# Step order in a two-block transformer kernel: one VectorE step per expert, gathered results in a split pair, ln2's norm ahead of the overflow branch

## What is computed

```python
for i in range(DEPTH):                      # first layers
    mix = token_mixers(x, ...)              # diff attention + dsa attention
    x = layer_norm(ALPHA * x + mix, ln1)
    ffn = hierarchical_moe(x, ...)          # 4 groups x 8 experts, 2 of one group per token
    ple = sigmoid(x @ w_ple_gate[i]) * (p[i] @ w_ple[i])
    x = layer_norm(ALPHA * x + ffn + ple, ln2)
for l in range(DEPTH):                      # second layers
    x = x + hybrid_mixer(rms_norm(x), ...)  # mla + moba + retention branches, gated
    x = x + squared_relu_mlp(rms_norm(x), w_up, w_down)
return rms_norm(x)
```

## Time and profile before

| | us |
|---|---|
| median of 3 runs (2105.99 to 2107.63) | 2106.68 |
| the profiled execution | 2105.99 |
| its span in the trace | 2104.2 |
| TensorE busy | 1964.6 |
| VectorE busy | 1410.0 |
| ScalarE busy | 1073.0 |
| GpSimd busy | 94.5 |

### The profile page before, as it was taken

The page is one execution under the profiler, slowest core; times in us unless marked ns, Lnnn a source line. Parts: engine busy times, 40 slices in busy tenths (PEclk is TensorE's granted clock), DMA queues, the critical chain, the costliest instruction groups (busy, mean ns, idle before and its releaser), DMA issues.

```text
span 2104.2 us, 31210 instructions
## 1 busy us (share of the span) xinstructions
PE 1964.6 (93%) x12616; PEld 1779.6 (85%) x12616; DVE 1410.0 (67%) x2278; ACT 1073.0 (51%) x1662; POOL 94.5 (4%) x88
## 2 busy tenths in 40 slices
PE   7889989999989799989999799999999899999998
PEld 6779878998877798779988689998999789998997
DVE  5765768888756766688887556667444666675444
ACT  4444446776634344467776254444444455444443
POOL 1000010000010000100000000000100000001001
PEclk9989899999989899899999799999999999999999
DMA  7425239999724243199998153344555443344552
GB/s 256 140 81 216 93 122 406 405 413 375 285 79 142 100 176 133 55 411 399 415 382 332 39 190 121 121 160 147 194 180 193 145 161 139 107 179 158 190 191 81
DMA packets 60152, 426.65 MB, mean 203 GB/s; under 512 B 6849, under 2 KB 7233, under 8 KB 9440
## 3 DMA queue, kind: packets, MB, share of 16 engines
q1 hardware_dynamic: 59040, 421.65, 53.2%
q0 software_dynamic: 384, 1.72, 0.3%
q10 hardware_dynamic: 576, 1.19, 0.2%
HBM read 423.49 MB, written 1.05 MB: 202 GB/s over the span
## 4 chain that ended last, share of the span: by engine, by line
PE 81%; DVE 12%; ACT 4%; issue 1%; POOL 1%; DMA 0%; DVEq 0%; ACTq 0%; POOLq 0%; SPq 0%
PE bank L968 65%; PE scp L968 11%; DVE WSl L1327 3%; PE bank L1071 2%; ACT WSh L1848 2%; PE bank L1203 1%; PE bank L1056 1%; PE bank L1098 1%; DVE sm L1464 1%; ACT SC L1885 1%; POOL sm L2061 1%; DVE scp L1462 0%; DVE TMP L1449 0%; DVE TMP L1441 0%; DVE sm L1447 0%
## 5 line engine op out<-in xcount | busy, mean ns | idle before, releaser
L1327 DVE TENSOR_TENSOR WSl<-ring,WSh 128x1024 fp32r<-128x1024 f32 (+3 forms) x508 | 589.5, 1205 | 236.9 <-ACT WSh L1848 236.0
L1848 ACT CAST WSh<-ring 128x1024 fp32r<-128x1024 f32 (+3 forms) x508 | 497.6, 1034 | 209.0 <-PE bank L968 119.0
L968 PE MATMUL bank<-XTh,WSh 128*128 128x256 f32 x1216 | 351.1, 289 | 13.8 <-DVE A L1499 13.6
L968 PE MATMUL bank<-XTl,WSh 128*128 128x256 f32 x1216 | 347.5, 286 | 0.0
L968 PE MATMUL bank<-XTh,WSl 128*128 128x256 f32 x1216 | 347.2, 286 | 0.0
L968 PE MATMUL bank<-WSh,FA 128*128 128x512 f32 (+1 forms) x848 | 302.1, 389 | 16.1 <-DVE FA L1748 16.1
L968 PE MATMUL bank<-WSl,FA 128*128 128x512 f32 (+1 forms) x680 | 263.3, 387 | 0.0
L968 PEld LDWEIGHTS bank<-XTh,WSh 128*128 128x128 f32 x1216 | 237.4, 195 | 15.1 <-issue 14.6
L968 PE MATMUL bank<-WSh,XTh 128*128 128x512 f32 (+4 forms) x576 | 227.2, 394 | 13.2 <-DVE WSl L1327 12.3
L968 PEld LDWEIGHTS bank<-XTl,WSh 128*128 128x128 f32 x1216 | 237.2, 195 | 0.2
L968 PEld LDWEIGHTS bank<-XTh,WSl 128*128 128x128 f32 x1216 | 236.8, 195 | 0.0
(11 more groups left out here) (270 smaller groups left out, 2933.0 us busy)
## 6 DMA issues: line engine op xcount, KB each, us to landing
ring<-wts SPq DMA_DIRECT2D x268, 1024.0 KB, 4.8
V<-wts SPq DMA_DIRECT2D x42, 1024.0 KB, 7.2
PT<-wts SPq DMA_DIRECT2D x29, 1024.0 KB, 8.0
H<-wts SPq DMA_DIRECT2D x24, 1024.0 KB, 7.9
GT<-wts SPq DMA_DIRECT2D x21, 1024.0 KB, 7.2
A<-wts SPq DMA_DIRECT2D x10, 1024.0 KB, 4.9
ring<-wts SPq DMA_DIRECT2D x3, 832.0 KB, 5.3
ring<-wts SPq DMA_DIRECT2D x2, 768.0 KB, 4.6
```

Source lines behind the costliest of these rows:

```text
L968: return nc.tensor.matmul(dst, lhsT, rhs, start=start, stop=stop)
L1327: nc.vector.tensor_tensor(lo[:, c], buf[:, c], hi[:, c].bitcast(F32), ALU.subtract).then_inc(*lo_done.inc(("block", i)))
L1848: nc.scalar.copy(hi[:, c], buffers[s.buffer][:, c]).then_inc(*hi_done.inc(("half", i, k)))
```

## The change

1. **Index steps.** Tile 0's 27 steps are put into `spare` right behind its relu, at pace 12 beside the dq columns ("beside the queries"); tile 1's follow, and what is left runs at pace 8 beside dk and dv.
2. **Attend.** A parameter `pre` emits fill blocks ahead of `between`; dsa uses (1, 2, 1) with pre=1 for (2, 2, 1), so one block moves ahead of the turn of diff's output. Diff's mix becomes a step of its own behind the first fill. All of diff's copies to PT are ScalarE's.
3. **Gather.** Expert 0's tokens are made in two halves, each behind four gather products; the zeroing step `clear` stands behind them, and TensorE, VectorE, ScalarE and GpSimd read the overflow flag there.
4. **Experts.** Pace 0; one `spare` step behind each `turn_h`. `gated` and `embedded` are halved (512 columns), which makes 14 steps, for experts 2 to 15. CT and the slot weights move from expert 7 to 10, the lending of GT and V0 from 8 to 17, V1 is recalled at the end.
5. **End of the experts.** `keep` is gone (the sum is made inside the overflow branch); YS's first half lies in a pair of split buffers, and one block less is split ahead.
6. **ln2.** `normed` stands ahead of `overflow`; inside the branch the norm is then made again.
7. **Second layer.** One `fill(1)` ahead of `turn_split("o1")`.

```diff
@@ take
-        ahead = [...][:2 + raw]
+        ahead = [...][:min(2 + raw, self.limit)]
@@ attend
-    def attend(self, att, l, heads, fills, between=None):
+    def attend(self, att, l, heads, fills, between=None, pre=0):
         self.add("soft", name=att, l=l, t=0, p=p, scp=scp)
+        self.fill(pre)
         if between is not None:
             between()
-        self.fill(fills[0])
+        if att == "diff":
+            self.fill(fills[0])
+            self.add("mix", name=att, l=l, t=0)
+        else:
+            self.fill(fills[0])
...
         self.add("soft", name=att, l=l, t=1, p=p, scp=scp)
+        if att == "diff":
+            self.add("mix", name=att, l=l, t=1)
@@ turn_p
-                owner = self.either()
+                owner = "act" if att == "diff" else self.either()
@@ first_layer
             self.add("relu", l=l, t=t, scp=scp, rl=rl[t])
+            self.spare.extend(("index", dict(l=l, t=t, rl=rl[t])) for _ in range(INDEX_STEPS))
             if t == 0:
+                self.pace = 12
                 self.columns("w_in", "dq", l, W1["dq"], 512, src)
-        self.spare.extend(("index", dict(l=l, t=t, rl=rl[t])) for _ in range(INDEX_STEPS) for t in range(T))
-        self.pace = 13
+        self.pace = 8
...
-        self.attend("dsa", l, 8, (2, 2, 1), diff_out)
+        self.attend("dsa", l, 8, (1, 2, 1), diff_out, pre=1)
...
             self.add("gather", l=l, c=k, u=self.bank("act"), owner="act", fa=xs)
+            if k % 4 == 3:
+                self.add("tokens_of", l=l, e=0, h=k // 4, u=len(self.owner))
         self.add("clear", l=l)
...
-        self.add("tokens_of", l=l, e=0, fa=fa)
         for e in range(NE):
...
-            if e == NE - 5:
-                self.recall("V1")
-                self.held["V1", l] = self.last_in("V1")
             if e == NE - 1:
                 self.recall("H", "V0")
-                self.add("keep", l=l)
-            if e == 8:
+            if e == 17:
                 self.lend("GT", ("dve", "embedded", l, 1))
                 self.lend("V0", ("dve", "gated_ple", l, 1))
...
+            if e == NE - 1:
+                ys = len(self.split_block)
+                self.split_block.append(("ys", l))
+                self.limit = 2
             if e == 2:
+                self.pace = 0
                 self.spare.extend(("weight", dict(l=l, t=t, c=c, o=o)) for t in range(T) for c in range(3))
-                self.spare.extend((kind, dict(l=l, t=t)) for t in range(T) for kind in ("gated", "embedded"))
-            if e == 7:
-                self.no_more_than(0)
+                self.spare.extend((kind, dict(l=l, t=t, c=c)) for t in range(T) for kind in ("gated", "embedded") for c in range(2))
+            if e == 10:
...
             self.add("turn_h", l=l, e=e, u=self.bank("dve"))
+            self.spread_out(1)
+        self.pace = 1
...
+        self.limit = 3
+        self.add("normed", name="ln2", l=l, n=D)
         self.add("overflow", l=l, u=len(self.owner))
-        self.add("normed", name="ln2", l=l, n=D)
@@ second_layer
             if t == 0:
+                self.fill(1)
                 fa = self.use("FA", "pe")
                 self.turn_split("o1", l, 4, o=self.now("O"), fa=fa)
@@ vector program, tokens of expert 0 (scalar program alike)
+                elif s.kind == "tokens_of" and s.e == 0:
+                    hi, lo = (XE[0][:, 4 * s.h:4 * s.h + 4, a:a + CAP] for a in (0, CAP))
+                    dve.wait_ge(act_done, "tokens", l, 0, s.h)
+                    nc.vector.tensor_tensor(lo, XG[:, 4 * s.h:4 * s.h + 4, 0:CAP], hi.bitcast(F32), ALU.subtract).then_inc(
+                        *dve_done.inc(("tokens", l, 0, s.h)))
@@ each engine's program, the flag
+                elif s.kind == "clear":
+                    dve.wait_ge(dve_done, "flag", l)
+                    yes = e.value_load(flag[0:1, 0:1], min_val=0, max_val=1)
@@ gpsimd program
-                elif s.kind == "keep":
...
-                    nc.gpsimd.tensor_tensor(XA, XT[0][:, :, :].bitcast(F32), XT[1][:, :, :].bitcast(F32), ALU.add).then_inc(
-                        *pool_done.inc(("kept", l)))
```

More of the change, by code:

```diff
@@ L180, in take @@
         raw = self.is_raw(spec)
-        ahead = [] if order is None else [j for j in range(i + 1, min(i + 4, len(order))) if not self.is_raw(order[j])][:2 + raw]
+        ahead = [] if order is None else [j for j in range(i + 1, min(i + 4, len(order))) if not self.is_raw(order[j])][:min(2 + raw, self.limit)]
         for j in [i] + ahead:
@@ L739, in build, with ys_of @@
         YC = A[:, KD * (SLOTS + CAP):2 * KD * (SLOTS + CAP)].rearrange("p (k s) -> p k s", k=KD)
-        YS = [[v.rearrange("p (j d) -> p j d", j=4) for v in pair]
-              for pair in ([x_[:, :, :].rearrange("p k s -> p (k s)") for x_ in XT], (FA[:, 0:2048], FA[:, 2048:4096]))]
+        def ys_of(s, n):
+            pair = (FA[:, 0:2048], FA[:, 2048:4096]) if n else [w[:, :] for w in WS[s.m % PAIRS]]
+            return [v.rearrange("p (j d) -> p j d", j=4) for v in pair]
         G = OHT[:, :].rearrange("p (t s) -> p t s", t=T)
@@ L826, in build @@
         VALUES = {"diff": ("dv", 1), "dsa": ("sv", 1), "mla": ("kv_up", 3), "moba": ("mv", 1), "ret": ("rv", 1)}
-        over = [{n: signal(f"over{l}_{n}") for n in ("pe", "dve", "act")} for l in range(DEPTH)]
+        over = [{n: signal(f"over{l}_{n}") for n in ("pe", "dve", "act", "pool")} for l in range(DEPTH)]
         over_in = [[signal(f"over{l}_in{i}", 16) for i in range(3)] for l in range(DEPTH)]
@@ L931, in overflow_vector @@
                     for h in range(2):
[L932 to L933 removed]
+                        nc.vector.bn_stats(MIX_STATS[:, t, 6 * h:6 * h + 6], X[:, t, 512 * h:512 * (h + 1)]).then_inc(*o_dve.inc())
+                    dve.wait_ge(o_dve)
+                    nc.vector.bn_aggr(mv[:, 2 * t:2 * t + 2], MIX_STATS[:, t, 0:12]).then_inc(*o_dve.inc())
+                dve.wait_ge(o_dve)
+                nc.vector.tensor_scalar(var, var, LN_EPS, None, ALU.add).then_inc(*o_dve.inc(("var", l)))
+                dve.wait_ge(over[l]["pool"], "pow", l)
+                for t in range(T):
+                    nc.vector.tensor_scalar(H[:, t, :], X[:, t, :], mv[:, 2 * t:2 * t + 1], mv[:, 2 * t + 1:2 * t + 2],
+                                            ALU.subtract, ALU.mult).then_inc(*o_dve.inc(("end", l)))
                 dve.wait_ge(o_dve, "end", l)
@@ L1788, in vector_program @@
                             add_y("moe", l, t, n, *([("scp", s.scp)] if n and t else []))
+                elif s.kind == "clear":
+                    dve.wait_ge(dve_done, "flag", l)
+                    yes = e.value_load(flag[0:1, 0:1], min_val=0, max_val=1)
                 elif s.kind == "overflow":
-                    dve.wait_ge(dve_done, "added", "moe", l, 1, 1)
-                    overflow_vector(e, l)
+                    overflow_vector(e, l, yes)
                 elif s.kind == "k_pe":
@@ L1980, in scalar_program @@
                                          bias=col("ln1_b", l, s.c)).then_inc(*act_done.inc(("bank", u)))
+                elif s.kind == "tokens_of" and s.e == 0:
+                    first[0] = 0
+                    for v in range(s.u - 4, s.u):
+                        act.wait_ge(emptied(v), "bank", v)
+                    act.wait_ge(pe_done, "gather", l, 4 * s.h + 3)
+                    nc.scalar.copy(XE[0][:, 4 * s.h:4 * s.h + 4, 0:CAP], XG[:, 4 * s.h:4 * s.h + 4, 0:CAP]).then_inc(
+                        *act_done.inc(("tokens", l, 0, s.h)))
                 elif s.kind == "tokens_of":
@@ L2088, in gpsimd_program @@
                     nc.gpsimd.memset(A[:, KD * (SLOTS + CAP):5120], 0.0).then_inc(*pool_done.inc(("YC0", l)))
-                elif s.kind == "keep":
-                    block_, raw = plan.held["V1", l]
-                    if raw:
-                        pool.wait_ge(pe_done, "read", block_)
-                    else:
-                        pool.wait_ge(lo_done, "block", block_)
-                    pool.wait_ge(dve_done, "ln1", l, 3)
-                    nc.gpsimd.tensor_tensor(XA, XT[0][:, :, :].bitcast(F32), XT[1][:, :, :].bitcast(F32), ALU.add).then_inc(
-                        *pool_done.inc(("kept", l)))
-                elif s.kind == "embedded":
+                elif s.kind == "embedded" and s.c == 0:
                     pool.wait_ge(dve_done, "affine", "ln1", l, 1)
```

100 lines of the change are left out of this document (56 added, 44 removed).

## The result

The changed kernel takes 2074.6 us (median of 4 runs, 2073.2 to 2078.3) where the kernel before takes 2107.2; the ratio is 0.9849, 95% interval 0.9837 to 0.9862. The forecast was 2069.7 in a range of 2052 to 2087. Run again later beside other kernels it took 2074.7 (ratio 0.9837, 0.9824 to 0.9851).

What follows compares the result with a forecast made beforehand. TensorE, busy 1964.6 of 2104.2 us, was taken as the bound, nearly every wait ending on VectorE. Terms summed to -37.0, giving a span of 2067.2 and, with run offsets, 2069.7 us; range 2052 to 2087.

Steps and rivals of the forecast that it cites:

- 7.3 us of clock: TensorE's half-clock time behind waits, counted as saved: 2.8 us a layer at O's turn, less 0.4, and 1.7 at o1.
- to about 5: Sign for the index steps: TensorE's wait at 102 us falls from 6.8 to about 5 us.
- single file: Index steps of one query tile alone, each waiting for its predecessor: about 0.12 us more per step.
- rival A: Index steps: single file costs nothing, waits under 2 us and half clock behind 102 us gone; 2059.7 us, chance 0.13.
- all diff copies of PT on ScalarE: 0: Diff's PT copies and late mix: earlier copies offset a later first turn; 0, bounds -2 to +2 us a layer.
- the 3 us at which the prediction would have called itself wrong: Sign of failure: a new wait of more than 3 us appears behind the diff mix.
- my 5.9: Expert loop before: four experts holding weight and gate steps took 36.42 us where 30.5 would do, so 5.9 lost.
- Rival B: Expert loop: the extra VectorE step is not hidden, 7.6 us a layer instead of 0.7; 2083.5 us, chance 0.13.
- one block less is split ahead; the next has 5 us: YS in split pair, at each layer's end: next block has 5 us before needed; +0.3 us a layer, +0.6 total.
- Rival C: Fills: the block before the turn is not split in time and TensorE waits for it; +12, 2081.7 us, chance 0.06.
- Rival D: Experts 2 to 17 with six buffers: transfers pace the loop, 9.0 us per expert, 45 us added; 2114 us, chance 0.06.
- the 0.9 that the prediction had set as a sign of being wrong: Sign of failure: the transfers' share falls below 0.9 inside the expert loop.

## Why the prediction was right, and where it was not

The sum was -37.0 us and the measured change of the span is -30.8. The sum holds 7.3 us of clock that I wrote out (5.6 at the turn of O, 1.7 at o1); the other 29.7 are waits and paces. Measured, TensorE's idle time fell by 30.7. The total is near partly by luck. Of the clock next to nothing shows in the span, since TensorE's busy time is the same, and an effect that I had not seen brought 3.8 in its place. One reading was off, though no term hangs on it: I wrote that nearly every wait of TensorE ends on VectorE, and by the whole list of waits 91 us do before and 40 end on ScalarE, 25.2 of them on its half of H; now it is 44 and 51. By steps:

**Index steps: forecast -3.4, measured -8.5 of idle time.** In layer 0 the wait fell from 6.79 to 4.43, 2.4 us where I had 1.7 and had written "to about 5". The price of single file was right too. VectorE's timeline of the changed kernel has a max/match round of the 256-wide tile alone at

```profile
93.01 0.43 DVE L1482 MAX8 sm<-TMP 128x8 f32<-128x256 f32 x1
...
94.00 0.43 DVE L1482 MAX8 sm<-TMP 128x8 f32<-128x256 f32 x1
```

0.99 us apart, where my working gives 0.72 + 2 x 0.12 = 0.96. The round of the other tile alone takes 0.72 (71.42 to 72.14), so the two cost 1.71 one behind the other and 1.17 interleaved. The rule of the Trainium skill that I weighed there (VectorE: DVE Perf Modes, The DRAIN you can't avoid) would have made it 0.72. The rows decide against it as I had used it: in these two traces a step that needs its predecessor's result costs more than one that doesn't. In layer 1 the wait is gone altogether, which is rival A's amount and not rival A's reason. The step that failed is "all diff copies of PT on ScalarE: 0". I priced the copies and did not see that they are counted: three calls fewer of a counter that runs through the whole program turn round the owners of ST's copies in layer 1. The three kernels with the order of the copies set by hand show it, at 4.2 to 4.4 us. Of the 5.1 us that were missing, 3.8 are the owner's (4.2 less 0.4 for the wait at the index scores of layer 1, 1.22 to 1.59), and 1.3 are the placing, worth 2.2 to 2.4 a layer where I had 1.7.

**Fill ahead of the turn of O, and the mix: forecast -12.0 and 0, idle time measured -7.1.** The waits for O are gone (7.2). The other waits from diff's scores to dsa's last product sum to 4.9 a layer before, and now to 5.7 in layer 0 and 4.3 in layer 1: nothing, as forecast, but with the single wait of 2.64 that is close to the 3 us at which the prediction would have called itself wrong.

**Clock: forecast -7.3 written out, measured -1.3 between the medians.** This is the term that was mis-sized most. The prediction's sign came true: the granted clock behind the turns of O is 1.00 now, and where the wait is, the low clock is behind it. The step that failed is to count that stretch as saved in the whole. Without the fill the wait and both stretches are back, and the time lost at the lower clock is 84.3 us (median of four runs) against 82.9 in the changed kernel, not 5.6 more. The sum was 77.8 to 88.6 us in the runs of the kernel before and 78.6 to 89.2 in those of the changed one; what keeps it there stays open. The same holds for a part that I did not see: before, the loop of experts had such a stretch (the granted clock is down at 358 and again at 944), and my term for the experts was read from spacings that held it. In the changed kernel such a stretch stands at the start of the loop instead, and there the spacing of the first two reduces, 8.06 in both layers before, is 9.68 in layer 0 (8.07 in layer 1; 10.66 and 9.63 in the second profile). I had no term for that.

**Tokens of expert 0: forecast -1.2, measured -2.2** (the waits there 4.4 and 4.5 before, 3.5 and 3.3 now; 3.4 and 4.3 in the second profile, which would be -1.2). The Trainium skill's rule on the port that VectorE and GpSimd share (SBUF — State Buffer, SBUF: two separate sides) did not bite here: VectorE's first half runs while GpSimd scales X and takes no longer than the second, which runs when GpSimd is done. GpSimd and VectorE in layer 1:

```profile
864.18 5.51 POOL L2146 TENSOR_SCALAR X<-X 128x1024 f32<-128x1024 f32 x2 [4.57 <-DVE X L1666]
...
868.38 0.43 DVE L1781 TENSOR_TENSOR FA<-A,FA 128x256 fp32r<-128x256 f32 x1 [4.29 <-ACT FA L2029]
...
872.04 0.43 DVE L1781 TENSOR_TENSOR FA<-A,FA 128x256 fp32r<-128x256 f32 x1 [3.23 <-ACT FA L2029]
```

**One step per expert: forecast -5.2 a layer, measured -5.3.** The spacings of experts 1 to 7 summed to 8.7 us over the steady 7.63 before; now experts 2 to 16 sum to 3.4, of which 2.6 are the turn of CT and 0.8 the fourteen steps (I had 0.7). The turn of CT is in both kernels (2.8 before) and was rightly left out of my 5.9. Rival B falls, and the run with two steps shows where it would have begun. **No keep: forecast -2.0 a layer, measured -2.4** (the two spacings 9.62 and 8.06 are 7.63 now).

**Norm and flag: forecast -2.3, measured -2.2 between the first profiles** (6.77 to 5.26, 6.08 to 5.39), and -2.9 with the second profile (5.05, 4.94). VectorE's gap of 1.26 is gone, and it writes H 2.5 us sooner behind its last statistic. TensorE gains 1.5 of them, for it now waits for ScalarE's half of H, and in layer 1 the first profile shows it waiting for its own issue, where the branch stands, and the second for VectorE's H. That layer 1 owes its 0.7 to the flag's read was not tried by itself.

**YS: forecast +0.6, measured +2.0**, in front of the second layers only. Here the step "one block less is split ahead; the next has 5 us" looked at TensorE's need of the block, and not at what the late casts stand in front of on ScalarE. The kernel with YS's pair reserved first shows the cause.

**Fill ahead of o1: forecast -4.3 with 1.7 of clock, measured -1.8** of idle time (1.31 gone, 0.4 more for GT, in two layers).

These add up: -8.5 - 7.1 - 2.2 - 10.9 (the waits in the two expert loops, 7.3 to 1.9 each; the 15.4 of the spacings above hold low-clock time too) - 2.2 + 2.0 - 1.8 = -30.7. Rival C falls: the block ahead of O was there in time. Rival D falls in its size, since the reduces of experts 2 to 15 stand 7.63 to 7.82 apart but for the turn of CT, and the transfers' share in the loops is 0.98 to 1.00, above the 0.9 that the prediction had set as a sign of being wrong. Its place was well chosen in part: short waits for landings appear at expert 17, and at the start of the loop.

## What to carry to other kernels

Where a planner hands out owners, banks or buffers by a counter, a change that takes one call away moves everything behind it. List who gets what before and after; here that was worth more than the part of the change it came from. Price a late operation by what stands behind it in its own engine's queue, and not only by who needs its result. And do not add the low-clock time behind a wait to that wait's price because the profile shows it there: here it came and went with the wait in every trace, and the sum over the span hardly followed. Compare the sums of several runs.

## What had not been expected of the hardware

One program loses a different amount at TensorE's lower clock in each run: 77.8 to 88.6 us in 27 runs of the kernel before, at times from 2103.0 to 2111.4 us. The time less that amount stays within 2020 to 2027. Some stretches move between profiles of one kernel while the mean granted clock is 0.960 in both. The one behind the turn of O is tied to its wait, in 6 of 6 places with the wait and 0 of 20 without, and taking it away lowered the sum by little. So a change of 2 us that the time can't show may still be read from TensorE's idle time, 108.9 and 108.5 in two profiles of one kernel; single waits in them differ by up to 1 us.
